# A decoder on one Trainium2 core: one projection from three split products to whole fp32 products, late weights in longer rows, modulation sums moved

## The reference

```
o = lax.map(per_seq, ...)                         # first attention, 16 heads of 64
h = h + o.reshape(B, T, 1024) @ a_w_out           # its output projection: the product that changes
h = h + sq_relu_mlp(rms_norm(h, g), w1, w2)       # relu(x @ w1)**2 @ w2, 1024 -> 4096 -> 1024
...
m = silu(c) @ w + b                               # modulation: 4 x 3072 sums over 1024
x = layer_norm(ALPHA*x + gate*diff_attention(...))
act = gelu(einsum('td,thkd->thk', xc, u[idx]))    # experts: one gathered row of u and v each
out = einsum('thk,thkd->td', g*act, v[idx])
```

## Time and profile before

| | us |
|---|---|
| median of 3 runs | 2437.72 (2437.59 to 2440.14) |
| the profiled execution | 2435.66 |
| its span, first to last instruction | 2433.8 |

### The profile page before, as it was taken

The page is one execution under the profiler, slowest core; times in us unless marked ns, Lnnn a source line. Parts: engine busy times, 40 slices in busy tenths (PEclk is TensorE's granted clock), DMA queues, the critical chain, the costliest instruction groups (busy, mean ns, idle before and its releaser), DMA issues.

```text
span 2433.8 us, 28455 instructions
## 1 busy us (share of the span) xinstructions
PE 2106.9 (87%) x9804; PEld 1352.1 (56%) x9804; DVE 1599.6 (66%) x3701; ACT 1138.1 (47%) x2760; POOL 639.6 (26%) x624
## 2 busy tenths in 40 slices
PE   7769999998999987897777989987998898888776
PEld 7648999876999986452223434432444443323222
DVE  5685677664778777867667467556648656676753
ACT  4354543534653434435445375434447444444543
POOL 0010011000001004544443234243324334434441
PEclk8869999999999988999999999999999999999998
DMA  6234588541569745999999999999999999999995
GB/s 226 87 104 147 174 280 283 173 165 41 171 215 361 268 148 190 396 419 419 419 420 407 392 412 413 395 418 420 395 389 369 398 381 420 420 420 420 420 421 212
DMA packets 139013, 768.23 MB, mean 316 GB/s; under 512 B 15232, under 2 KB 18048, under 8 KB 73088
## 3 DMA queue, kind: packets, MB, share of 16 engines
q0 software_dynamic: 87552, 587.24, 59.6%
q1 hardware_dynamic: 50608, 177.81, 20.7%
q10 hardware_dynamic: 720, 1.51, 0.2%
HBM read 765.45 MB, written 1.05 MB: 315 GB/s over the span
## 4 chain that ended last, share of the span: by engine, by line
PE 51%; DMA 25%; DVE 11%; ACT 8%; issue 3%; POOL 1%; SPq 0%; ACTq 0%; POOLq 0%; DVEq 0%
DMA arena<-experts,arena 24%; PE bank L860 12%; PE bank L513 9%; PE bank L515 9%; PE bank L514 9%; PE bank L895 6%; DVE arena L2120 3%; DMA wring<-w_stream 2%; ACT L1335 1%; ACT arena L1340 1%; ACT arena L1339 1%; ACT arena L1157 1%; DVE arena L1678 1%; PE bank L613 1%; DVE wlo L1566 1%
## 5 line engine op out<-in xcount | busy, mean ns | idle before, releaser
L860 PE MATMUL bank<-arena 128*128 128x512 f32 x2048 | 983.2, 618 | 168.0 <-ACT arena L1340 167.6
L2120 DVE CUSTOM_DVE_ANT_0 arena<-arena 128x1024 f32<-128x1024 f32 x512 | 631.2, 1234 | 468.4 <-DMA arena<-experts,arena 467.4
L480 POOL DMA_INDIRECT arena<-experts,arena x512 | 560.0, 1094 | 862.6 <-PE bank L860 820.2
L860 PEld LDWEIGHTS bank<-arena 128*128 128x128 f32 x2048 | 374.1, 194 | 730.3 <-ACT arena L1340 374.8
L1566 DVE TENSOR_TENSOR wlo<-wring,whi 128x1024 fp32r<-128x1024 f32 x224 | 272.9, 1224 | 168.1 <-ACT whi L1083 167.3
L1083 ACT CAST whi<-wring 128x1024 fp32r<-128x1024 f32 x236 | 246.3, 1048 | 275.4 <-PE bank L515 274.0
L1335 ACT ACTIVATE arena<-arena 128x1 f32<-128x1 f32 x512 | 102.9, 201 | 472.3 <-DVE arena L2120 470.5
L1340 ACT ACTIVATE arena<-tab,arena 128x128 f32<-128x128 f32 x512 | 205.5, 401 | 16.7
L513 PE MATMUL bank<-hTh,whi 128*128 128x256 f32 (+1 forms) x640 | 192.3, 300 | 22.0 <-DVE hTl L1575 18.9
L466 POOL DMA_DIRECT2D arena<-ada_w x64 | 34.0, 531 | 664.7 <-DVE adaM L1613 646.5
L514 PE MATMUL bank<-hTl,whi 128*128 128x256 f32 (+1 forms) x640 | 187.3, 293 | 0.0
(11 more groups left out here) (304 smaller groups left out, 3039.1 us busy)
## 6 DMA issues: line engine op xcount, KB each, us to landing
wring<-w_stream SPq DMA_DIRECT2D x332, 512.0 KB, 4.7
arena<-ada_w POOLq DMA_DIRECT2D x64, 512.0 KB, 5.3
alibi<-ada_w POOLq DMA_DIRECT2D x32, 512.0 KB, 5.4
arena<-experts,arena POOLq DMA_INDIRECT x512, 14.2
xT<-xT_in SPq DMA_DIRECT2D x1, 1088.0 KB, 5.0
alibi<-alibi_in ACTq DMA_DIRECT2D x1, 1024.0 KB, 5.0
outT<-xT SPq DMA_DIRECT2D x2, 512.0 KB, 13.5
tab<-tab_in SPq DMA_DIRECT2D x1, 831.0 KB, 6.5
```

The lines of the kernel that those rows point to most:

```text
L480: pool.indirect_dma_start(g_ring[:, r], None, experts[n // (2 * PEER_HEADS)], bass.IndirectOffsetOnAxis(idx[:, s // SLOTS % 2, s % SLOTS:s ...
L860: last = mm(banks[2 * t + b][:, :], diag[:, r], g_ring[:, r, D + b * TILE_N:D + (b + 1) * TILE_N], start=s % SLOTS == 0, stop=s % SLOTS == ...
L2120: v.tensor_tensor_reduce(g_ring[:, r, 0:D], g_ring[:, r, 0:D], hrow[:, t], 1.0, 0.0, ALU.mult, ALU.add, act8[:, r:r + 1]).then_inc(dot_don ...
```

## The change

Four edits.

1. The first attention's output goes unsplit into `hT` (ACT, one copy per part), `out_proj` multiplies tiles 5 and 6 by `whole_chunk`: 8 fp32 matmuls per chunk, weights straight from `wring`. The splits of tiles 5 and 6 (8 on ACT, 8 on DVE) and the six `out_lo` of this attention are gone; PE's values wait for `ot_copied` in place of `ot_split`. `split_no` renumbers the remaining splits.
2. No modulation sum stands in the attention. Three move to the first MLP's second tile, twelve to the shared key and query projections.
3. The late weights are laid out by halves of the contraction: half a tile is one DMA of 1 MB with rows of 8 KB, with a semaphore of its own; 48 DMAs in place of 96.
4. `half_tile` waits for its own half alone and raises `lin_done` by two after each half; SP loads a half as soon as the same half two tiles back is used.

```diff
+        def split_no(g, c):
+            return CPT * (g - 2 * (g > G_AOUT + 1)) + c + 1
+        def late_half(g, half):
+            return wring[:, g % 2, 2 * half:2 * half + 2].rearrange("p c k n -> p (c k n)")
...
-            for g in range(N_LOADS):
+            for g in range(G_QKV):
...
+            for g in range(G_QKV, N_LOADS):
+                tile = w_stream[g if g < N_TILES else g - BESIDE].rearrange("c p k n -> (c p k n)").rearrange(
+                    "(h p m) -> h p m", h=2, p=P)
+                for half in range(2):
+                    sp.wait_ge(lin_done, CPT * (g - 2) + 2 * half + 2)
+                    sp.dma_start(late_half(g, half), tile[half]).then_inc(late_landed[g % 2][half], 16)
...
-                            pe.wait_ge(ot_split, 2 * r + u)
+                            pe.wait_ge(ot_copied, 2 * r + u)
...
+            def whole_chunk(g, c, dst):
+                pe.wait_ge(w_landed[g % 2][c], 16 * (g // 2 + 1))
+                for kc in range(KC):
+                    last = mm(dst, wring[:, g % 2, c, kc], hT[:, kc], start=kc == 0, stop=kc == KC - 1)
+                last.then_inc(lin_done, 1)
...
-                        chunk(g, c, banks[c][:, 0:n], rhs)
+                        if rhs:
+                            chunk(g, c, banks[c][:, 0:n], rhs)
+                        else:
+                            whole_chunk(g, c, banks[c][:, 0:n])
...
-                if half == 0:
-                    for c in range(CPT):
-                        pe.wait_ge(w_landed[g % 2][c], 16 * (g // 2 + 1))
-                for kc in range(4 * half, 4 * half + 4):
-                    last = mm(dst, lhs[:, kc], wring[:, g % 2, :, kc], start=kc == 0, stop=kc == KC - 1)
-                if half:
-                    last.then_inc(lin_done, CPT)
+                pe.wait_ge(late_landed[g % 2][half], 16 * ((g - G_QKV) // 2 + 1))
+                w = late_half(g, half)
+                for k in range(4):
+                    last = mm(dst, lhs[:, 4 * half + k], w[:, k * TILE_N:(k + 1) * TILE_N], start=half == 0 and k == 0,
+                              stop=half == 1 and k == 3)
+                last.then_inc(lin_done, CPT // 2)
...
-                            nc.scalar.copy(hTh[:, piece, q0:q0 + nq], src).then_inc(ot_copied, 1)
+                            nc.scalar.copy(hT[:, piece, q0:q0 + nq], src).then_inc(ot_copied, 1)
...
-                split_hi(g + 1, c)
-                split_hi(g + 1, c + 1)
+                if g + 1 < G_AOUT:
+                    split_hi(g + 1, c)
+                    split_hi(g + 1, c + 1)
             pair_root(4)
             attention(0)
-            split_his(G_AOUT + 1)
...
-                        if k < KC - 1:
+                        if k < KC - 1 and g != G_AOUT:
                             split_lo(g + 1, c)
...
-                parts = ((0, 0, 0, 0, 1, 1, 1, 2, 2, 2, 2, 1, 1, 1, 1), (0, 0, 0, 0, 0, 0, 0, 0, 0, 0, 0))[layer]
...
-                    for _ in range(parts[n]):
-                        ada_part()
-                    if n >= 3:
+                    if layer and n >= 3:
                         out_lo(n - 3)
...
-                two(0, 1, True)
+                two(0, 1, True, 0 if layer else 3)
...
-            split_los(5)
...
             for x in range(8):
                 split_lo(G_BK + x // CPT + 1, x % CPT)
-                if x % 2:
-                    ada_part()
+                ada_part()
```

More of the change, by code:

```diff
@@ L347, in build @@
         sk_landed = sem("sk_landed")
+        late_landed = [[sem(f"late_landed{s}_{h}") for h in range(2)] for s in range(2)]
         w_landed = [[sem(f"w_landed{s}_{c}") for c in range(CPT)] for s in range(2)]
@@ L764, in _ @@
             attention(0)
[L765 to L766 removed]
+            pe.wait_ge(ot_copied, 6)
+            out_proj(G_AOUT, T, None, 0)
             mlp(0, 0)
@@ L1711, in out_lo @@
                 def out_lo(n):
-                    r, x = quads[layer][n]
+                    r, x = quads[1][n]
                     q0, nq = ROWS[r]
-                    if layer == 0:
-                        units = [(2 * r + u, slice(4 * u, 4 * u + 4)) for u in range(2)] if x == 3 else []
-                    else:
-                        units = [(outs(1, n), slice(2 * x, 2 * x + 2))]
-                    for unit, piece in units:
-                        if layer:
-                            src = banks[7][:, :].rearrange("p (c b q) -> p c b q", c=2, b=2)
-                            dve.wait_ge(ot_copied, unit + 1)
-                            for b in range(2):
-                                half = slice(64 * b, 64 * b + 64)
-                                last = v.tensor_tensor(hTl[half, piece, q0:q0 + nq], src[half, :, b],
-                                                       hTh[half, piece, q0:q0 + nq].bitcast(F32), ALU.subtract)
-                            last.then_inc(ot_split, 1)
-                        else:
-                            src = banks[7][:, :].rearrange("p (c q) -> p c q", c=4)[:, :, 0:nq]
-                            lo_part(hTl[:, piece, q0:q0 + nq], src, hTh[:, piece, q0:q0 + nq], ot_copied, unit + 1, ot_split)
+                    src = banks[7][:, :].rearrange("p (c b q) -> p c b q", c=2, b=2)
+                    piece = slice(2 * x, 2 * x + 2)
+                    dve.wait_ge(ot_copied, outs(1, n) + 1)
+                    for b in range(2):
+                        half = slice(64 * b, 64 * b + 64)
+                        last = v.tensor_tensor(hTl[half, piece, q0:q0 + nq], src[half, :, b],
+                                               hTh[half, piece, q0:q0 + nq].bitcast(F32), ALU.subtract)
+                    last.then_inc(ot_split, 1)
                 for n in range(N + 3):
@@ L1757, in hidden_lo, with two @@
                     lo_part(flat(h1l), hidden(p, m), flat(h1h), h1_hi, p * (2 * CPT) + (32 * layer + m + 1), h1_split)
-                def two(p, s, before):
+                def two(p, s, before, beside=0):
                     for c in range(CPT):
+                        if c < beside:
+                            ada_part()
                         m = CPT * s + c
@@ L2293 @@
     assert w_stream.shape[0] == N_TILES
+    late = w_stream[G_QKV:].reshape(-1, CPT, P, 2, KC // 2, P).transpose(0, 3, 2, 4, 1, 5)
+    w_stream[G_QKV:] = late.reshape(w_stream[G_QKV:].shape)
     ada_w = i["ada_w_2"].reshape(4, D, 3 * D).transpose(0, 2, 1).reshape(96, P, D)
```

26 lines of the change are left out of this document (13 added, 13 removed).

## The result

The changed kernel takes 2411.12 us (median of 6 runs, 2407.03 to 2414.37) against 2437.65 for the kernel before beside it: ratio 0.990, 95% interval 0.988 to 0.992, so 26.5 us less. Its profiled execution took 2410.36 us with a span of 2408.5, each 25.3 less than before.

What follows compares the result with a forecast made beforehand. PE, or what feeds it, was taken to bound the early program, bytes the expert stage. 2435.66 - 4.6 - 12.0 + 4.5 - 8 = 2415.6, plus 2.06 for the median: 2417.6 us, range 2404 to 2431.

Steps and rivals of the forecast that it cites:

- Splits of tile 5: Between last rotation and first score: four splits alone on DVE go, saving 4.6 us (4.0 to 4.7).
- The loop: First attention: removed sums and low halves 11.3 us, less 2.3 for ACT, plus 3.0 for unblocked queues: saves 12.0 (9 to 15).
- The projection: First output projection: 64 fp32 matmuls take 29.4 us instead of 24.9 at full clock, costing 4.5 us (4.3 to 8.9).
- The sums elsewhere: First MLP and key and query projections: moved modulation sums hide behind PE, cost 0, at most 14 us.
- The late weights: Expert stage: longer rows and earlier half-tile requests together save 8 us, bounds 0 and some 20.
- (a): Late weights in expert stage: fewer rows carry the same bytes, so only the rate could change; 1 us, bounds 0 and 3.
- Part (b): Late weights: half tiles requested earlier fill DMA dips, 5 us, and end a PE wait, 2 us.
- The paragraph on sharing: Gathers beside late weights: 8 KB rows might double the weights' share, first half landing after 5 to 8 us, or change nothing.
- The slower rival: Late tiles: 8 KB weight rows delay gathers 1.25 us per tile, costing 30 us; 2455.6 us, chance 0.05.
- Nothing late: Expert stage: the late-weight change gains nothing because PE is busy through the dips; 2425.6 us, chance 0.28.
- Much late: Expert stage: half tiles end PE's waits and most first MBs fall into dips, 20 us; 2405.6 us, chance 0.13.
- Taken back: Attention loop gains 9, projection starting at half clock costs 8.9, late weights give nothing; 2433.0 us, chance 0.06.

Runs made afterwards that it cites:

- edits 1 and 2 alone: Against the kernel before: whole fp32 first output projection, no modulation sums in its attention, late weights unchanged; 2419.73 and 2420.47 us, ratios 0.993 and 0.995.
- edits 3 and 4 alone: Against the kernel before: late weights by halves in rows of 8 KB, early stages unchanged; 2424.39 us, ratio 0.995.

## Why the forecast came out as it did

**Splits of tile 5** (forecast -4.6): right. The first mask stands 0.7 us behind the last rotation's end, 4.54 us sooner when the later start is taken off.

**The loop** (-12.0, measured -10.75, of which 1.6 are the clock): the sum was near, its pieces were not. Up to the first mask of the third group, 151.73 before and 143.36 after, the loop won 5.0 us where my pieces gave 7.5. It is as much as the removed pieces of the chain (four sums and two low halves), but not because the blocked queue was worth nothing. From 138.63 to 147.22 before, 132.97 to 139.43 after, the masks came 2.1 us closer where the chain credits 0.5; I had 3. So 1.7 of my 2.5 us came, and the mask waited for PE's scores, as I had said. The next step, 4.51 us before with two sums of 2.27 in it, shrank only by 0.6: PE, at half clock, took 6.0 us for values, scores, transposes and scores from 137.38 to 143.36, and the mask waited for those. I had counted both sums there in full. From there to the last group's mask at 160.56 (172.99 before) it won 4.1 where my pieces gave 1.9: the quads shrank to 3.35 and 3.74 us where I had 3.6, and 1.6 us is PE at full clock for transposes and values, which I had not counted. Behind it 1.7 against 2.5. That the sum came near is in part luck.

**The projection** (+4.5, measured +4.33, or 4.5 by the start of the norm's sums behind it): right. The 64 matmuls take 29.60 us to their end, at a granted clock of 1.00 in this execution and in the same 29.60 us in every profiled run that has them.

**The sums elsewhere** (0): right. In the window of the keys PE is busy for 98.00 of 98 us; DVE went from 54.9 to 66.4 (69 forecast). What was won at the first norm's sums in the MLP, 9.6 us, stood at 9.0 at the mixers' first turn. By the medians of the runs with edits 1 and 2 alone the early part is worth 13 to 18 us, by the profiled executions 7 to 9.5; the forecast of 12.1 lies between, and these runs don't decide it closer, since a kernel's own runs lie 10 us apart.

**The late weights** (-8, measured -16.3 in the profiled pair, 13.0 between the means of the mixers' times without and with the late edits, 12 to 13 by the median of edits 3 and 4 alone): the direction was right, the step that failed is (a). I had "Fewer rows: the bytes are the same, so only the rate could change", 1 us with bounds 0 and 3. Rows of 8 KB alone are worth 21 us over rows of 4 KB in the new layout, 16 over the old one. I took their price from a stretch without a dip, where nothing can be won. What the runs show is that longer rows bring a tile in sooner and take the weights' DMAs off the chain. That they thereby fill the dips is my reading of it. The first 60 us of the mixers fit it. Before, from 1320, then after, from 1310 us, columns as in the earlier trace rows:

```profile
1320.00:1380.00 60.00, 56.30 (x160) 27.91 (x160) 38.62 (x95) 28.46 (x76) 16.89 (x15) 0.98 0.98 378
```

```profile
1310.00:1370.00 60.00, 57.21 (x167) 27.73 (x166) 38.64 (x95) 28.69 (x76) 17.54 (x17) 1.00 1.00 411
```

That is 4.7 us of transfer time in 60. Over the mixers the missing time falls from 37.5 to 21.0 us, 16.5, and the stretch is 16.3 shorter. With the bytes equal these two must agree, since the stretch is bytes at 420 GB/s plus what the dips leave out; it says how much, not why. PE's own idle time shows a part: 5.0 us of waits for weights are gone, and 10.9 us at L867 for DVE's `hfT`, two waits at 1528 and 1928 us. The second kind is 11.7 us with whole tiles of 4 KB rows, 2.5 with 8 KB and none in the changed kernel; what links it to the weights is not shown. Part (b), 7 us for half tiles, was sized too low as well (15.4 from the whole tiles with 4 KB), and the two being two ways into the same dips, they must not be added; the rest, some 21 us, stays, in dips such as 296 and 306 GB/s.

**The paragraph on sharing** held the mechanism that the sum did not use. It expected a first half after 5 to 8 us if longer rows raise the share, and it is 9.0. The Trainium skill (DMA: Bandwidth & Descriptors, Queues, rings and completion order) has the engines take turns by packets of several descriptors; by that a longer descriptor gives a larger share, and from 4 to 16 KB the runs agree (20, 15, 13 us for the slowest tile, 19.0, 13.9, 11.6 for the middle one); from 2 to 4 KB only the slowest tile moves much. The packet of at most 4096 B that the same page prefers (SWDGE vs HWDGE vs iDMA), taken as a limit for longer rows too, would leave the share alone from 4 KB on; the fall from 19.9 to 14.9 and 12.8 us speaks against that reading. The slower rival rested on the same sharing. Its premise came true in part, gathers land 1 to 2 us later, and its conclusion did not: the mixers became shorter. That eight slots hold enough in flight is my explanation, which no run tested.

**The rivals.** "Nothing late" falls with 0.995 (0.993 to 0.997) for edits 3 and 4 alone. "Much late", 20 us from half tiles in dips, was the nearest in the profile and had 0.13. "Taken back" needed a projection at half clock, which no run showed. Of the signs to look for, all came but two in part: the first halves land within 10.6 us, not 10, and everything stands 9 us sooner, not 12.

**The sum.** By the profiled pair the early part is 3.1 us short of the forecast and the late part 8.3 over it. Two misses of opposite sign left the profiled time 5.2 us and the median 6.5 us under the forecast; that the total came closer than the late part did is luck.

## What to carry to other kernels

Where two streams of DMAs are in flight together, try longer rows for the one that a consumer waits for: beside gathers with rows of 8 KB, weights came in sooner with each step from 4 to 16 KB. Price that where the rate dips, not where it is full, and look for the stream on the chain, since PE's idle time of 5.0 us hid 32.8 us of it. Two measures against the same idle time don't add, so run each alone before adding them. Work that leaves a pipelined loop is worth what the chain held of it, up to the next engine at its own clock, so compare the granted clock of both before you credit an edit.

## What the runs showed of the hardware that I had not expected

- Rows taking turns one by one, an estimate, come near the longest landing times from 4 KB on. With gather rows of 8 KB, weight rows of r KB would have a share of r / (r + 8); 2 MB at 410 GB/s alone is 5.1 us, so 25.6, 15.3, 10.2 and 7.7 us at 2, 4, 8 and 16 KB. With one constant of 4.7 us, fitted, that is 30.3, 20.0, 14.9 and 12.4 against maxima of 37.1, 19.9, 14.9 and 12.8. For 2 KB it fails both ways: the slowest is later than 30.3, and the middle tile, whole after 20.7 us, hardly later than with 4 KB (19.0).
- The same instructions, after the same wait of 3.43 us, ran at full clock in one execution (2.94 us) and at half in another (5.36), and everything behind moved by 2.4 us. Five of fourteen profiled executions had it. At the third group another 1.6 us hang on the clock. A difference of 2 us between two profiles of such a kernel is not yet one between the kernels.
- Eight whole fp32 matmuls of 272 columns take 3.65 us (29.23 / 8, start to start), the 24 split products 3.07 (24.54 / 8, without the stall of 0.36): 19% more on PE buys off eight splits on each of ACT and DVE.
